# Values centred by the product that turns them, in a two-block kernel with a recurrent mixer

## The reference

```python
def step(S, inp):
    r_t, w_t, k_t, v_t, a_t, b_t = inp
    sa = jnp.einsum('bhvk,bhk->bhv', S, a_t)
    S = S * w_t[:, :, None, :] + sa[..., None] * b_t[:, :, None, :] + v_t[..., None] * k_t[:, :, None, :]
    y = jnp.einsum('bhvk,bhk->bhv', S, r_t)
    return S, y
...
y = _wkv7_scan(...)
mean = jnp.mean(y, axis=-1, keepdims=True)
var = jnp.mean(jnp.square(y - mean), axis=-1, keepdims=True)
y = ((y - mean) * lax.rsqrt(var + GN_EPS)).reshape(B, T, D_RWKV)
y = (y * ln_w.astype(f32) + ln_b.astype(f32)).astype(p.dtype)
bonus = jnp.sum(r_h * k_h * r_k, axis=-1, keepdims=True) * v_h
return (y + bonus.reshape(B, T, D_RWKV)) * g
```

## Time and profile before

| | |
|---|---|
| median of 3 runs | 2732.66 us |
| lowest and highest | 2726.9 and 2739.32 us |
| span of the profiled execution | 2733.5 us (its time is recorded only as this span) |
| PE busy | 2651.5 us, 97% |
| DVE, ACT, POOL busy | 66%, 47%, 5% |

### The profile page before, as it was taken

One profiled execution on the slowest core, in us unless ns is written; L12 is line 12 of the kernel. 1 busy time (PEld: TensorE's weight loads), 2 busy tenths in 40 slices (PEclk: granted clock), 3 DMA queues, 4 the chain that ended last, 5 costly groups with the idle time before them and its releaser, 6 DMA issues.

```text
span 2733.5 us, 48562 instructions
## 1 busy us (share of the span) xinstructions
PE 2651.5 (97%) x17888; PEld 2193.5 (80%) x17888; DVE 1808.5 (66%) x2619; ACT 1272.6 (47%) x1787; POOL 145.8 (5%) x148
## 2 busy tenths in 40 slices
PE   5799999999999999999999999999999999999998
PEld 0466667788888888888888888888888888888887
DVE  0455555567777777655567777777678888886554
ACT  1333333345555555444433356554555555554443
POOL 1001111420000000010100000000100000000000
PEclk8799999999999999999999999999999999999999
DMA  9877776254555555555555544445555555555553
GB/s 400 324 305 280 288 282 248 97 185 155 186 188 186 187 187 185 191 196 213 200 193 186 185 170 154 167 171 187 186 183 187 187 188 187 186 184 198 203 199 136
DMA packets 84243, 554.82 MB, mean 203 GB/s; under 512 B 8496, under 2 KB 8624, under 8 KB 19888
## 3 DMA queue, kind: packets, MB, share of 16 engines
q1 hardware_dynamic: 83424, 550.21, 54.7%
q10 hardware_dynamic: 720, 3.21, 0.3%
HBM read 551.29 MB, written 2.10 MB: 202 GB/s over the span
## 4 chain that ended last, share of the span: by engine, by line
PE 82%; issue 9%; DMA 4%; DVE 3%; ACT 1%; POOL 0%; DVEq 0%; SPq 0%; ACTq 0%; POOLq 0%
PE bank L568 37%; PE bank L569 19%; PE banks L568 14%; PE banks L569 7%; DMA raw<-in_stream_dram 4%; PE bank L615 1%; DVE wlo L1614 1%; DVE yb L2273 0%; DVE yb L2276 0%; PE banks L1099 0%; PE banks L1119 0%; PE banks L767 0%; PE banks L1108 0%; POOL bm L2343 0%; DVE ft L2279 0%
## 5 line engine op out<-in xcount | busy, mean ns | idle before, releaser
L1614 DVE TENSOR_TENSOR wlo<-raw,whi 128x1024 fp32r<-128x1024 f32 x846 | 1028.0, 1224 | 206.1 <-ACT whi L1166 200.6
L568 PE MATMUL bank<-act,whi 128*128 128x512 f32 x3056 | 1100.2, 402 | 1.7 <-DVE x L1994 1.2
L1166 ACT ACTIVATE whi<-raw 128x1024 fp32r<-128x1024 f32 x846 | 878.1, 1051 | 390.8 <-PE bank L569 307.0
L569 PE MATMUL bank<-act,wlo 128*128 128x256 f32 x3056 | 856.8, 280 | 0.5 <-issue 0.5
L568 PEld LDWEIGHTS bank<-act,whi 128*128 128x128 f32 x3056 | 573.9, 188 | 161.2 <-issue 20.2
L568 PE MATMUL banks<-act,whi 128*128 128x512 f32 x1664 | 596.6, 401 | 6.0 <-DVE act L1664 6.0
L569 PEld LDWEIGHTS bank<-act,wlo 128*128 128x128 f32 x3056 | 577.6, 189 | 1.9 <-issue 1.7
L568 PE MATMUL bank<-ff,whi 128*128 128x512 f32 x1408 | 493.2, 393 | 1.3 <-DVE wlo L1614 1.3
L569 PE MATMUL banks<-act,wlo 128*128 128x256 f32 x1664 | 469.9, 282 | 0.0
L569 PE MATMUL bank<-ff,wlo 128*128 128x256 f32 x1408 | 392.9, 279 | 0.0
L568 PEld LDWEIGHTS banks<-act,whi 128*128 128x128 f32 x1664 | 315.9, 190 | 84.4 <-issue 6.4
(11 more groups left out here) (269 smaller groups left out, 1882.0 us busy)
## 6 DMA issues: line engine op xcount, KB each, us to landing
raw<-in_stream_dram SPq DMA_DIRECT2D x519, 1024.0 KB, 4.8
x<-in_x_dram SPq DMA_DIRECT2D x1, 2048.0 KB, 13.6
lora_w<-in_lora_dram SPq DMA_DIRECT2D x1, 1536.0 KB, 12.1
pool_w<-in_pool_w_dram ACTq DMA_DIRECT2D x1, 1024.0 KB, 6.2
out_dram<-x SPq DMA_DIRECT2D x2, 512.0 KB, 2.8
out_dram<-x ACTq DMA_DIRECT2D x2, 512.0 KB, 3.0
catt<-in_att_dram ACTq DMA_DIRECT2D x1, 576.0 KB, 3.2
par<-in_params_dram SPq DMA_DIRECT2D x1, 541.5 KB, 3.7
```

The costliest lines, as they stand in the source:

```text
L568: nc.tensor.matmul(tile_bank(t), wh, flat(pair[:, kt]), start=starts and n == 0, stop=False)
L569: mm = nc.tensor.matmul(small_half(t), wl, pair[:, kt, 0], start=False, stop=stops and last)
L1166: nc.scalar.activation(whi[:, k % RING], raw[:, r % RING, 8 * (k % 2):8 * (k % 2) + 8], ACT.Copy)\
L1614: nc.vector.tensor_tensor(wlo[:, k % RING], raw[:, r % RING, 8 * (k % 2):8 * (k % 2) + 8], whi[:, k % RING].bitcast(F32), ALU.subtract).th ...
```

## The change

Three things change. A constant matrix `centring` (identity minus 1/64 in each head's block) is made once by DVE at the start, and in `turn_step` the four value pieces of each group are turned by an ordinary float32 product with it instead of a transpose; the eight key pieces are still transposed. At the end of a group the mean product, DVE's `centre` and their semaphores are gone: ACT's square waits for `y_ready` itself, and the wait that `mean_step` held moves to `var_step`. In `spread`, the product with the identity becomes a transpose.

```diff
+        centring = rec("centring", [P, P])
             def spread(dst, cols, signal):
                 for b in range(2):
-                    mm = nc.tensor.matmul(dst[:, b * P:(b + 1) * P], cols[:, b:b + 1].to_broadcast([P, P]), ident, start=True, stop=True)
+                    mm = nc.tensor.transpose(dst[:, b * P:(b + 1) * P], cols[:, b:b + 1].to_broadcast([P, P]), ident)
                 mm.then_inc(signal, 1)
...
-                    src = vraw[:, p, cols] if w == 2 else bk[:, p, w, cols]
-                    mm = nc.tensor.transpose(work[n // 4][:, (n % 4) * P:(n % 4 + 1) * P], src, ident)
+                    dst = work[n // 4][:, (n % 4) * P:(n % 4 + 1) * P]
+                    if w == 2:
+                        mm = nc.tensor.matmul(dst, vraw[:, p, cols], centring[:], start=True, stop=True)
+                    else:
+                        mm = nc.tensor.transpose(dst, bk[:, p, w, cols], ident)
...
-            def mean_step(g):
-                pe.wait_ge(y_ready, g + 1)
-                if g == NGROUP - 1:
-                    pe.wait_ge(mod_ready, 6)
-                else:
-                    pe.wait_ge(kk_scaled, g + 2)
-                head_sum(t2).then_inc(mean_sum, 1)
...
             def var_step(g):
                 pe.wait_ge(var_in, g + 1)
+                if g == NGROUP - 1:
+                    pe.wait_ge(mod_ready, 6)
+                else:
+                    pe.wait_ge(kk_scaled, g + 2)
                 head_columns(flat(zmat[:])).then_inc(var_sum, 1)
...
             def variance_in(g):
-                act.wait_ge(centred, g + 1)
+                act.wait_ge(y_ready, g + 1)
                 nc.scalar.activation(flat(zmat[:]), flat(t2[:]), ACT.Square).then_inc(var_in, 1)
...
-            dve.wait_ge(derived, 3)
+            dve.wait_ge(res_loaded, 16)
+            nc.vector.scalar_tensor_tensor(out=centring[:], in0=headones, scalar=-1.0 / HEAD, in1=ident, op0=ALU.mult, op1=ALU.add)\
+                .then_inc(derived, 1)
+            dve.wait_ge(derived, 4)
...
-            def centre(g):
-                dve.wait_ge(mean_sum, g + 1)
-                nc.vector.scalar_tensor_tensor(out=flat(t2[:]), in0=aux[:, :], scalar=-1.0 / HEAD, in1=flat(t2[:]), op0=ALU.mult,
-                                               op1=ALU.add).then_inc(centred, 1)
```

More of the change, by code:

```diff
@@ L378, in blocks_program @@
         s_mm, s_ready, y_mm, y_ready = sem("s_mm"), sem("s_ready"), sem("y_mm"), sem("y_ready")
-        mean_sum, centred, var_in, var_sum, gn_std, gn_out, mixed = (
-            sem("mean_sum"), sem("centred"), sem("var_in"), sem("var_sum"), sem("gn_std"), sem("gn_out"), sem("mixed"))
+        var_in, var_sum, gn_std, gn_out, mixed = (
+            sem("var_in"), sem("var_sum"), sem("gn_std"), sem("gn_out"), sem("mixed"))
         pool_z, pool_mm, pool_out = sem("pool_z"), sem("pool_mm"), sem("pool_out")
@@ L930, in recurrence_step @@
                 then = {1: (z_step, (1,)), 2: (z_step, (2,)), 3: (z_step, (3,)), 4: (z_step, (4,)),
-                        5: (z_step, (5,)), 6: (av_step, ()), 8: (u_step, (1,)), 9: (r_step, (2,)), 11: (u_step, (3,)),
-                        12: (mean_step, ())}
+                        5: (z_step, (5,)), 6: (av_step, ()), 8: (u_step, (1,)), 9: (r_step, (2,)), 11: (u_step, (3,))}
                 (first if g == NGROUP - 1 else then)[14] = (var_spread, ())
@@ L1903, in recurrence @@
                     y_out(g)
-                    centre(g)
                 if n == 13:
@@ L2141, in _ @@
             link(nc.vector.tensor_tensor(gs[:, 0], pcol("norm_f_g", 0, KT), pcol("norm_mix_g", 0, KT), ALU.mult))
-            dve.wait_ge(derived, 5)
+            dve.wait_ge(derived, 6)
             dve.sem_inc(constants, 1)
```

## The result

The changed kernel takes 2709.99 us (median of 6 runs, of which five lie from 2704.53 to 2713.95; the sixth, at 4449.37 with a mean granted clock of 0.645, is left out of the ratio) against 2729.78 us for the kernel before, measured beside it. The ratio is 0.9921, with a 95% interval of 0.99 to 0.9942. The profiled execution has a span of 2708.9 us against 2733.5, 24.6 less.

What follows compares the result with a forecast made beforehand. PE's instruction order was taken as the bound, except the last group's end, bound by the chain from DVE's sum. 3.0 + 3.0 - 0.45 + 2.1 = 7.65 us off 2732.66 gave 2725.0 us; range 2714 to 2736.

Steps and rivals of the forecast that it cites:

- x4 likewise two steps, 0.23: Spread at norm x4, in PE's dense stream: two records fewer, saving 0.23 us.
- First three groups: Ends of the first three recurrence groups: mean product and part of the wait for the square go, 3.0 us saved.
- the turning's 0.45: Value pieces turned by two-record products: 0.45 us more PE time, charged once since gaps hide it after the first group.
- DVE's `centre` cost PE nothing of its own: First three groups: DVE's centring and the wait ahead of it did not delay PE, so removing them earned nothing extra.
- Last group: End of the fourth group: shorter chain to the variance product gives 1.9 us, up to 4.9 with full clock; 3.0 taken.
- The row nearest to the new situation: Last group's old clock row: PE idles before 519 us both ways, a reason to stay nearer the lower end, 1.9.
- Spreads: Norm spreads at x0, x1, x2, x4 and x5: half the records as transposes, 2.1 us saved, lower bound 1.5.
- (a): Half-clock stretches at 519 us and in the third group do not occur: 12.6 us saved, 2720.1 us; chance 0.15.
- (d): Without the mean product the clock falls in more groups, about 3 us each; three more give 2734 us; chance 0.07.
- (b): The DMA weight stream swallows the first three groups' 3.0 us: 2728.0 us; chance 0.10.
- (c): Transposes leave the clock low, such as behind x2's spreads: 1.7 us a fall, 2726.7 or 2728.4 us; chance 0.08.
- (e): Turning products cost their full 1.8 us and x0's saving is used up: 2726.9 us; counted within the forecast's 0.60.

Runs made afterwards that it cites:

- x4_only: The kernel before with only the two spread products of x4 turned into transposes: 2718.45 us, ratio 0.9969.
- x4_product: The changed kernel with only the two transposes at x4 turned back into products: 2720.17 us, ratio 0.9968 to the kernel before.
- after_again: The changed kernel measured and profiled once more, nothing altered: 2713.95 us, ratio 0.9941 to the kernel before.

## Why the prediction was wrong

**The step that failed** is the sum's silence on everything that the change leaves alone. It priced the four spread records at x4 by their steps, "x4 likewise two steps, 0.23", and took every other stretch of PE as what it was before. The records did save 0.23 us. But what follows them is an up projection of some 480 us of PE without a gap, and the records in front decide which of two rhythms it takes. P P led to the long one in 6 profiles of 6, T T to the short one in 7 of 7. x4_only and x4_product show that those two instructions carry 9 us, alone in the kernel before (8.9 by the medians) and undone in the changed one (9.2 behind x4, between its profile and that of after_again). The other part of the miss is the draw behind x1, another 9.2 us in the profile of the first comparison. In after_again, which drew the long rhythm there, the profile gained 18.2 us up to the end of the second up projection instead of 24.0. The medians of the two comparisons, 19.8 and 15.3 us apart, mix such draws on both sides; how much of each is the draw can't be read from them.

**The sum itself** held: 8.3 us were measured with x4 undone, 7.65 forecast (7.4 without x4's share); the ratio's interval allows 4.4 to 13.4. The agreement is partly luck: the terms themselves gave about 1 us more than forecast, and the rhythm behind x2, which the forecast did not have, took 2.3 back. The terms were partly right for other reasons. *First three groups*: 3.0 less the turning's 0.45 were forecast, 3.7 measured (3.5 by the means). The turning did cost nothing behind the first group, and beyond that the 0.47 wait for L1818 that should have absorbed it went away; of the two issue stalls in group 3, one (1.0) is absent from both profiles of the changed kernel. "DVE's `centre` cost PE nothing of its own" may be where this fails, since without it DVE reaches L1818 earlier; that was not tried alone. *Last group*: 3.0 forecast, of which 1.1 for the clock. The chain gave 1.90, the lower bound, and the low stretch stayed whole: 6.8 us at half clock in both kernels. The row nearest to the new situation had said so. From the first value record of its turn to its variance product the group is 55.3 us in all nine kernels with centring against 58.0 on average in the eleven without, 2.8 less, so about 0.9 came from earlier in the group in place of the clock's 1.1. The clock's share was not nothing in every execution. In after_again the stretch was 3.4 us long (0.57 over 510 to 513 us, 0.86 over 513 to 516), and the output projection began 11.04 us behind the variance product's start instead of 12.50. Without centring it was 10.2 us long in three profiles of eleven and 6.8 in eight. From the group's turn to x1 the means lie 3.2 us apart. *Spreads*: 2.1 forecast, 2.0 measured.

**Rivals.** (a), the clock spared: wrong at 519, where it fell in all 20 profiles, for half as long in one of them. In group 3 it mostly is spared (9 of 11 to 2 of 9), but group 2 takes the falls instead, which is the mechanism of (d) in one group. (b) did not occur: PE's wait for the stream between 190 and 525 us is 1.4 us in all. (c) did not occur: the clock falls around x2 in both kernels (0.79 over 1384 to 1392 us before, 0.72 over 1368 to 1374 after, ahead of the spreads at 1375.75), and behind x4 it is 1.00. The Trainium skill's page "TensorE: Matmul & The Clock Gate", Part 4, says that transposes do not count as busy in the same way. These spreads show no fall from it, but they are two to four records among products and test it only weakly. (e) was wrong in both its parts: the turning did not cost 1.8, and x0's spread saved 0.53 us.

**The range** was too narrow because it was built from spreads of times alone. The kernel before held the warning: in one trace the same pair took 0.347 us in one stretch at clock 1.00 and 0.353 in others. I had read PE as busy 97% and so as fixed.

One gap remains: why one sequence leads to one rhythm. A shift of the code by three instructions, the kind of the last record, the record count and the instruction count are refuted. The length of the gap alone is too, unless it acts on a scale finer than 0.01 us, since T T T and T P or P T have nearly the same. Behind x2 the long rhythm came in all 9 kernels with centring and in 3 of 11 without; it costs 2.3 us there (3.4 in after_again, where the next stretch was long too), and what links it to the groups is not known. Whether the other engines, which read and write the same buffers in step with PE, take part was not tested.

## What to carry to other kernels

Where PE is busy without a gap, count its records in equal windows of several stretches before costing an edit. If the same instructions at the same clock take two different steps, an edit of two instructions at the entry of such a stretch can win or lose far more than its own time. Read the result from the same instruction of both traces, stretch by stretch, and repeat the profile of one kernel, before the gain is put down to the edit. Here two transposes at one norm were worth 9 us and the whole rest of the change 8.

## What the runs showed of the hardware

Back-to-back products of float32r tiles, of 512 and 256 columns, with their weight loads ran at 0.3467, 0.3500 or 0.3533 us a pair at a granted clock of 1.00. The first and the last held over the more than 1300 pairs of an up projection and through its loop, the middle one over the some 680 pairs of both down projections, in every kernel. At x4 two transposes in a stream that ran at 0.3467 left it there in 7 profiles of 7, and two float32 products turned it to 0.3533 in 6 of 6; elsewhere two transposes turned such a stream long three times of four.

The Trainium skill's page "TensorE: Matmul & The Clock Gate", section "Back-to-back issue gap", gives N/2.4 + 2.5 ns for an isolated product at full clock, by which a pair would take 0.325 us as an estimate, and says that a sustained stream of 512-column products is faster than that. These traces have the pair slower than the estimate, and show more than one value for one stream.
